# A block inverse in an RWKV-7 and window-attention layer: 64x64 products on all four tiles of TensorE

## What is computed

```python
def wkv_step(S, inp):
    r_t, w_t, k_t, v_t, a_t, b_t = inp
    sa = jnp.einsum('bhij,bhj->bhi', S, a_t)
    S = S * w_t[:, :, None, :] + sa[..., None] * b_t[:, :, None, :] + v_t[..., None] * k_t[:, :, None, :]
    return S, jnp.einsum('bhij,bhj->bhi', S, r_t)
```

## Time and profile before

| | us |
|---|---|
| median of three runs | 1687.83 (1686.51 to 1688.15) |
| the profiled execution | 1689.05 |
| its span, first to last instruction | 1687.0 |
| one step of the heads, j = 3 | 44.3 |
| all nine steps, x of j = 0 to the mean of the last tile | 392.16 |

### The profile page before, as it was taken

The page is one execution under the profiler, slowest core; times in us unless marked ns, Lnnn a source line. Parts: engine busy times, 40 slices in busy tenths (PEclk is TensorE's granted clock), DMA queues, the critical chain, the costliest instruction groups (busy, mean ns, idle before and its releaser), DMA issues. The chain is left out here.

```text
span 1687.0 us, 37211 instructions
## 1 busy us (share of the span) xinstructions
PE 1564.6 (93%) x15821; PEld 1471.5 (87%) x15821; DVE 777.4 (46%) x1310; ACT 579.6 (34%) x1126; POOL 125.4 (7%) x131
## 2 busy tenths in 40 slices
PE   6999998689899998839999999999999999999998
PEld 6999997477777777629988999999999999999998
DVE  5123332567677766362233443333444333344444
ACT  6443211455555555452124222332222233322211
POOL 3000000222222222020000000000000000000000
PEclk9999998799999999959999999999999999999999
DMA  6111111000000000034002111101111111011003
GB/s 177 38 48 39 49 37 33 7 4 3 3 3 3 3 3 3 4 94 126 25 12 89 48 28 51 51 27 47 50 50 36 39 50 50 25 50 50 25 1 106
DMA packets 82531, 66.82 MB, mean 40 GB/s; under 512 B 14929, under 2 KB 74507, under 8 KB 82411
## 3 DMA queue, kind: packets, MB, share of 16 engines
q1 hardware_dynamic: 79939, 64.26, 12.9%
q10 hardware_dynamic: 2408, 0.76, 0.2%
q0 software_dynamic: 64, 0.03, 0.0%
HBM read 59.66 MB, written 5.44 MB: 39 GB/s over the span
## 5 line engine op out<-in xcount | busy, mean ns | idle before, releaser
L100 PE MATMUL bank<-mix_hi,uw_hi 128*128 128x384 f32 (+1 forms) x768 | 255.7, 333 | 6.6 <-DVE uw_lo L1903 6.6
L100 PE MATMUL bank<-u_hi,dw_hi 128*128 128x384 f32 (+1 forms) x768 | 255.5, 333 | 3.6 <-DVE dw_lo L1908 3.6
L1923 DVE TENSOR_TENSOR hT<-hT,bank 128x384 f32<-128x384 f32 (+1 forms) x384 | 197.3, 536 | 131.7 <-PE bank L102 131.7
L101 PE MATMUL bank<-mix_lo,uw_hi 128*128 128x384 f32 (+1 forms) x768 | 255.1, 332 | 0.0
L102 PE MATMUL bank<-mix_hi,uw_lo 128*128 128x384 f32 (+1 forms) x768 | 255.0, 332 | 0.0
L101 PE MATMUL bank<-u_lo,dw_hi 128*128 128x384 f32 (+1 forms) x768 | 253.7, 330 | 0.0
L102 PE MATMUL bank<-u_hi,dw_lo 128*128 128x384 f32 (+1 forms) x768 | 253.6, 330 | 0.0
L1915 DVE TENSOR_TENSOR u_lo<-xn,u_hi 128x384 fp32r<-128x384 f32 (+1 forms) x96 | 52.0, 542 | 308.8 <-ACT u_hi L1874 308.8
L100 PE MATMUL bank<-x_hi,w_hi 128*128 128x384 f32 (+1 forms) x480 | 160.2, 334 | 0.1
L101 PE MATMUL bank<-x_lo,w_hi 128*128 128x384 f32 (+1 forms) x480 | 158.4, 330 | 0.0
L102 PE MATMUL bank<-x_hi,w_lo 128*128 128x384 f32 (+1 forms) x480 | 158.3, 330 | 0.0
(11 more groups left out here) (272 smaller groups left out, 2476.2 us busy)
## 6 DMA issues: line engine op xcount, KB each, us to landing
w_stage<-in_w_up SPq DMA_DIRECT2D x32, 512.0 KB, 4.5
d_stage<-in_w_down SPq DMA_DIRECT2D x32, 512.0 KB, 4.2
w_stage<-in_w_in SPq DMA_DIRECT2D x16, 512.0 KB, 3.9
proj<-in_x SPq DMA_DIRECT2D x9, 512.0 KB, 5.1
xs<-in_x SPq DMA_DIRECT2D x9, 512.0 KB, 4.5
w_stage<-in_w_in SPq DMA_DIRECT2D x8, 256.0 KB, 4.3
w_stage<-in_w_out SPq DMA_DIRECT2D x8, 256.0 KB, 3.1
w_stage<-in_w_out SPq DMA_DIRECT2D x16, 128.0 KB, 4.0
```

Source lines behind the costliest of these rows:

```text
L100: pe.matmul(out, hi, x_hi, start=first, stop=False)
L101: pe.matmul(out, hi, x_lo, start=False, stop=False)
L1923: dve.tensor_tensor(hT[:, m, c:c + n], hT[:, m, c:c + n], bank[j % 6][:, 0:n], ALU.add).then_inc(dn_add.sem, 1)
```

## The change

For half of the heads, a product's result is put on the other half of the partitions than the one it contracts over. So 8 of the 16 matmuls of a product use the two tiles off the array's diagonal, and TURN says which pairs of heads change the half at each level. turned_half, slot and tile_order keep track of where each head then lies and put straight and crossing matmuls in turn. p1 and e1 don't cross (TURN[1] is zero); p2 to p5, e2 to e4 and t1 to t5 do.

A crossing product writes two banks, one for each half that it contracts over (row), 256 columns in each: p(l) to columns 0 to 255 of banks 0 and 1, e(l) to columns 256 to 511 of the same banks, t(l) to banks 2 and 3. Masks and copies then read two banks in one instruction. All other results get other banks, and out_var moves behind extend(4).

```diff
-        bank = [whole.enter_context(nc.psum_tensor(f"bank{b}", [P, 512], F32)) for b in range(8)]
+        psum = whole.enter_context(nc.psum_tensor("psum", [P, 8, 512], F32))
+        bank = [psum[:, b] for b in range(8)]
...
+SCHEDULE = [("x", 6, 0), ("zw", 7, 1), ("za", 4, 1), ("p1", 0, 0), ("tr_a", 5, 0), ("tr_b", 6, 0), ("e1", 0, 0), ("t1", 2, 0),
+            ("s0a", 7, 0), ("s0b", 4, 0), ("vt", 5, 0), ("p2", 0, 0), ("tr_k", 6, 0), ("tr_v", 7, 0), ("e2", 0, 0), ("t2", 2, 0),
+            ("mean", 4, -1), ("p3", 0, 0), ("kk", 5, 1), ("e3", 0, 0), ("t3", 2, 0), ("pt0", 6, 0), ("pm0", 7, 0), ("p4", 0, 0),
+            ("s1a", 4, 0), ("s1b", 5, 0), ("e4", 0, 0), ("t4", 2, 0), ("var", 6, -1), ("o0", 7, 0), ("p5", 0, 0), ("z", 4, 0),
+            ("t5", 2, 0), ("gate", 5, -1), ("pt1", 6, 0), ("pm1", 7, 0), ("wu0", 0, 0), ("wu1", 1, 0), ("ab0", 2, 1), ("ab1", 3, 1),
+            ("q0", 4, 0), ("q1", 5, 0), ("tg0", 6, 0), ("tg1", 7, 0), ("y0", 0, 0), ("y1", 1, 0), ("st0", 2, 0),
+            ("ak0", 3, 1), ("ak1", 4, 1), ("o1", 5, 0), ("st1", 2, 0), ("bon", 3, 1)]
...
+TURN = {1: (0, 0, 0, 0), 2: (0, 0, 1, 1), 3: (0, 1, 1, 0), 4: (1, 1, 0, 0), 5: (1, 0, 0, 1), 6: (0, 0, 0, 0)}
+def turned_half(l, k, e):
+    return e ^ TURN[l][k // 2]
+def slot(crossing, k, row):
+    if not any(crossing):
+        return k
+    return 4 * row + [m for m in range(8) if crossing[m // 2] == crossing[k // 2]].index(k)
+def tile_order(crossing):
+    if not any(crossing):
+        return [(k, e) for k in range(8) for e in range(2)]
+    sides = [[k for k in range(8) if crossing[k // 2] == side] for side in range(2)]
+    return [(ks[n], e) for n in range(4) for ks in sides for e in range(2)]
+def t_crossing(l):
+    return tuple(a ^ b for a, b in zip(TURN[l], TURN[l + 1]))
...
+    def chain_out(name):
+        if name == "p1":
+            return bank[0]
+        if name == "e1":
+            return bank[1]
+        if name[0] == "t":
+            return psum[:, 2:4, 0:256]
+        return psum[:, 0:2, 0:256] if name[0] == "p" else psum[:, 0:2, 256:512]
...
             def product(j, l):
                 f.await_read(pe, "x" if l == 1 else f"e{l - 1}", j)
-                diagonal(j, f"p{l}", lambda k: Ab(j)[:, k, 0], lambda k: X[:, k])
+                f.await_room(pe, f"p{l}", j)
+                for k, e in tile_order(TURN[l]):
+                    mm = pe.matmul(chain(f"p{l}", k, turned_half(l, k, e), e), Ab(j)[half(e), k, 0], x_at(l, k, e), start=True, stop=True)
+                mm.then_inc(f.full(f"p{l}"), 1)
             def extend(j, l):
                 f.await_read(pe, f"p{l}", j)
                 if l == 1:
                     pe.wait_ge(xt1_ok.sem, xt1_ok.n(j))
+                    f.await_read(pe, "bon", j)
+                    if j > 0:
+                        f.await_read(pe, "y1", j - 1)
                 else:
                     f.await_read(pe, f"t{l - 1}", j)
                 if l < 5:
-                    diagonal(j, f"e{l}", lambda k: XT[:, k], lambda k: Pm[:, k])
-                diagonal(j, f"t{l}", lambda k: Pm[:, k], lambda k: XT[:, k])
+                    f.await_room(pe, f"e{l}", j)
+                    for k, e in tile_order(TURN[l]):
+                        mm = pe.matmul(chain(f"e{l}", k, e, turned_half(l, k, e)), xt_at(l, k, e), pm_at(l, k, e), start=True, stop=True)
+                    mm.then_inc(f.full(f"e{l}"), 1)
+                f.await_room(pe, f"t{l}", j)
+                for k, e in tile_order(t_crossing(l)):
+                    mm = pe.matmul(chain(f"t{l}", k, turned_half(l + 1, k, e), turned_half(l, k, e)), pm_at(l, k, e), xt_at(l, k, e),
+                                   start=True, stop=True)
+                mm.then_inc(f.full(f"t{l}"), 1)
...
                 scores(j, 1)
+                extend(j, 4)
                 if j > 0:
                     out_var(j - 1)
-                extend(j, 4)
                 attend(j, 0)
...
             def extended(j, l):
                 if l < 5:
-                    copy_out(f"e{l}", j, X[:], k8(f.bank(f"e{l}")[:]))
-                copy_out(f"t{l}", j, XT[:], k8(f.bank(f"t{l}")[:]))
+                    copy_out(f"e{l}", j, X[:] if l == 1 else X4, spread(f"e{l}", chain_out(f"e{l}")))
+                copy_out(f"t{l}", j, XT4, spread(f"t{l}", chain_out(f"t{l}")))
...
+                    dve.tensor_tensor(dst[:].rearrange("p (b n) t -> p b n t", b=2), spread(name, chain_out(name)),
+                                      lvl[:, l].unsqueeze(1).unsqueeze(1).to_broadcast([P, 2, 4, 64]), ALU.mult).then_inc(f.read(name), 1)
```

More of the change, by code:

```diff
@@ L87, in build_program @@
         s = dict(sem=sem, sb=sb, proj=proj, ident=ident, ones=ones, ones_bd=ones_bd, par=par, eps=eps, last_p=last_p,
-                 w_stage=w_stage, bank=bank, col=col, bias=bias,
+                 w_stage=w_stage, bank=bank, psum=psum, col=col, bias=bias,
                  wkv_out=Count(nc.alloc_semaphore("wkv_out")),
@@ L566, in scalar @@
         act.wait_ge(self.st_t.sem, self.st_t.n(0))
-        act.activation(v["Hs"][:].rearrange("p a b -> p (a b)"), bank[5][:, 0:256], ACT.Copy)
-        act.activation(v["ksm"][:], bank[4][:, 0:80], ACT.Copy).then_inc(self.st_c.sem, 1)
+        act.activation(v["Hs"][:].rearrange("p a b -> p (a b)"), bank[6][:, 0:256], ACT.Copy)
+        act.activation(v["ksm"][:], bank[3][:, 0:80], ACT.Copy).then_inc(self.st_c.sem, 1)
     def tensor(self, pe):
@@ L579, in tensor @@
         for p in range(4):
-            pe.transpose(bank[5][:, 64 * p:64 * p + 64], self.states[:, P * p:P * p + P], ident[0:64, 0:64])
-        pe.transpose(bank[4][:, 0:80], self.ck, ident[0:80, 0:80]).then_inc(self.st_t.sem, 1)
-SCHEDULE = [("x", 4, 0), ("zw", 6, 1), ("za", 7, 1), ("p1", 0, 0), ("tr_a", 3, 0), ("tr_b", 5, 0), ("e1", 1, 0), ("t1", 2, 0),
[6 rows of a table removed]
+            pe.transpose(bank[6][:, 64 * p:64 * p + 64], self.states[:, P * p:P * p + P], ident[0:64, 0:64])
+        pe.transpose(bank[3][:, 0:80], self.ck, ident[0:80, 0:80]).then_inc(self.st_t.sem, 1)
+SCHEDULE = [("x", 6, 0), ("zw", 7, 1), ("za", 4, 1), ("p1", 0, 0), ("tr_a", 5, 0), ("tr_b", 6, 0), ("e1", 0, 0), ("t1", 2, 0),
[6 rows of a table added]
+TURN = {1: (0, 0, 0, 0), 2: (0, 0, 1, 1), 3: (0, 1, 1, 0), 4: (1, 1, 0, 0), 5: (1, 0, 0, 1), 6: (0, 0, 0, 0)}
[12 more added lines that the diff above has]
+    return tuple(a ^ b for a, b in zip(TURN[l], TURN[l + 1]))
 class Fills:
@@ L636, in loop_heads @@
     kst, vtk, vmt, vms, ksm, Lg, PT, PTm, nm, sm, sk = (v[k] for k in "kst vtk vmt vms ksm Lg PT PTm nm sm sk".split())
+    psum = s["psum"]
+    X4, XT4 = (t[:].rearrange("p (b n) t -> p b n t", b=2) for t in (X, XT))
     f = Fills(sem, bank)
@@ L670, in window, with chain, x_at, pm_at @@
         return cols(0) if j == 0 else cols(j, P, -64 if e == 0 else 0)
+    def chain(name, k, out, row):
+        n = slot(t_crossing(int(name[1])) if name[0] == "t" else TURN[int(name[1])], k, row)
+        at = chain_out(name)[half(out)]
+        return at[:, 64 * n:64 * n + 64] if len(at.shape) == 2 else at[:, row, 64 * (n % 4):64 * (n % 4) + 64]
+    def chain_out(name):
[6 more added lines that the diff above has]
+        return psum[:, 0:2, 0:256] if name[0] == "p" else psum[:, 0:2, 256:512]
+    def x_at(l, k, e):
+        return X[half(e), k if l == 1 else slot(TURN[l - 1], k, turned_half(l - 1, k, e))]
+    def pm_at(l, k, e):
+        return Pm[half(turned_half(l, k, e)), slot(TURN[l], k, e)]
+    def xt_at(l, k, e):
+        return XT[half(turned_half(l, k, e)), k if l == 1 else slot(t_crossing(l - 1), k, turned_half(l - 1, k, e))]
+    def spread(name, ap):
+        return k8(ap) if name in ("p1", "e1", "x") else ap.rearrange("p b (n t) -> p b n t", n=4)
     r_in = lambda j: proj[:, 0:4, cols(j)]
@@ L807, in apply @@
                         for e in range(2):
-                            mm = pe.matmul(f.bank(f"wu{g}")[half(e), P * (k % 4):P * (k % 4) + P], XT[half(e), k], AZ[half(e), k],
+                            mm = pe.matmul(f.bank(f"wu{g}")[half(e), P * (k % 4):P * (k % 4) + P], xt_at(6, k, e), AZ[half(e), k],
                                            start=True, stop=True)
@@ L1255, in level @@
                 f.await_full(dve, name, j)
-                dve.tensor_tensor(dst[:], k8(f.bank(name)[:]), lvl[:, l].unsqueeze(1).to_broadcast([P, 8, 64]),
-                                  ALU.mult).then_inc(f.read(name), 1)
+                if name in ("x", "p1"):
+                    dve.tensor_tensor(dst[:], k8(f.bank(name)[:]), lvl[:, l].unsqueeze(1).to_broadcast([P, 8, 64]),
+                                      ALU.mult).then_inc(f.read(name), 1)
+                else:
+                    dve.tensor_tensor(dst[:].rearrange("p (b n) t -> p b n t", b=2), spread(name, chain_out(name)),
+                                      lvl[:, l].unsqueeze(1).unsqueeze(1).to_broadcast([P, 2, 4, 64]), ALU.mult).then_inc(f.read(name), 1)
             def product(j, l):
```

## The result

The changed kernel took 1664.95 us in the median of four runs (1662.17 to 1671.20), the kernel before 1687.73 beside it: ratio 0.9873, 95% interval 0.985 to 0.9895. The forecast was 1659, with 1645 to 1674. The profiled execution is the fastest run, 1662.17 with a span of 1660.0. In it the loop over the nine tiles lasts 363.49 us instead of 392.16: 28.67 less, where the sum said 28.5. So the walk through the steps held in this execution, the fastest of the four, and the question is why the other runs are up to 9 us longer than this one.

A forecast was written before the change was run, and what follows sets the result against it. TensorE was nearest to a bound, in a chain with VectorE and ScalarE. Savings of 1.7 + 7 x 3.2 + 4.4 = 28.5 us took the median of 1687.83 to 1659, range 1645 to 1674.

The forecast's parts named there:

- e2: Product on TensorE in step j = 3, released by VectorE's mask of p2: forecast to start 0.47 us earlier.
- e4: Product on TensorE in step j = 3, starting 0.06 us behind its mask's end: forecast gain 2.84 us.
- the sum: Saving over the nine tile steps: 1.7 first, 7 x 3.2 middle, 4.4 last, 28.5 us in all.
- the walk: Step j = 3 followed wait by wait: of 5.6 us saved on TensorE, 3.2 shorten the step, 2.4 become idle time.
- The banks: New dealing of results to banks in the loop: the new waits are met early, cost 0.
- The two-bank reads: Masks and copies reading two banks in one instruction: taken as 0, at most 1.05 us a step, up to 9 in all.
- out_var's move: Output product placed behind t4: e4 starts 0.06 instead of 0.67 us behind its mask's end.
- (a): Rival: all of TensorE's saving in the loop lands, 50.8 us, giving 1637; chance 0.07.
- (d): Rival: crossing and straight tiles don't overlap when alternating, or two-bank reads eat the gain: about 1687 us; chance 0.04.
- (c): Rival: the clock stays low from the transposes to the gate product's end, 3.4 us slower a step, 1715; chance 0.05.
- (b): Rival: the clock falls after the longer gap before the transposes, 1.5 us a step, 12 in eight, 1671; chance 0.18.
- my case: The prediction's own outcome for the whole kernel: 1659 us, with 1650 to 1668 around it; chance 0.66.

The follow-up runs named there:

- after: The changed kernel itself, no further edit, first measurement: 1664.95 us, ratio 0.9873; its profiled execution is the fastest run, 1662.17 us.
- before_again: The kernel before the change, no edit, one more run: loop 391.52 us, q at 34.29 to 34.36 us in steps 1 to 7.
- no_cross_var: Changed kernel with no product crossing and out_var ahead of extend(4) again, so only the banks are new: 1690.78 us, ratio 1.0011.
- var_back: Changed kernel with out_var put back ahead of extend(4), all else as changed: 1671.31 us, ratio 0.9893.
- straight_first: Changed kernel with each product's eight straight matmuls issued first, then its eight crossing ones: 1679.85 us, ratio 0.9945.
- after_again: The changed kernel measured a second time, no edit: 1669.45 us, ratio 0.9889.
- after_third: The changed kernel measured a third time, no edit: 1667.99 us, ratio 0.9867.
- reorder: Changed kernel with the logits' maximum behind the mask of p2, and softmax work ahead of the next tile's preparation: 1659.12 us, ratio 0.9816.
- filler: Changed kernel with two matmuls on constants in front of the wait before pt0 in every step: 1668.42 us, ratio 0.9885.
- split_logits: Changed kernel with VectorE's maximum of the logits moved behind the mask of p2: 1660.11 us, ratio 0.9829.

## Why the prediction was right, and where it was off

**The walk.** Gains at the points of step 3, each the time of the earlier trace rows less that of after, less the 7.46 us by which the step itself starts earlier:

| point | forecast | measured |
|---|---|---|
| e2 | 0.47 | 0.37 |
| p3 | 1.41 | 1.30 |
| Pm of p3 | 1.87 | 1.72 |
| pt0 (idle there) | 1.87 (2.3) | 1.73 (2.23) |
| Pm of p4 | 2.23 | 2.17 |
| e4 | 2.84 | 2.69 |
| pt1 (idle there) | 3.2 (1.6) | 2.97 (1.52) |
| q | 3.2 | 3.08 |

The small loss sets in at e2: it starts 0.15 behind the end of its mask (450.28 + 0.69 to 451.12), where it started 0.06 behind before, and the same 0.15 stands at e4. I had carried the 0.06 over. By stretches the sum is 2.1 for the first step (forecast 1.7), 7 x 3.14 for the middle (7 x 3.2) and 4.6 for the last (4.4). That it comes within 0.2 of 28.5 is in part luck. Of three profiles of the changed kernel this is the one without a fall, and the first step's 2.1 hangs on when the clock comes up: before_again has 41.79 there instead of 43.07, against which the gain is 0.8.

**The terms at nothing.** The banks: right (no_cross_var: q unchanged). The two-bank reads: right (691 and 592 ns; the earlier trace rows have 0.69 and 0.60), so the upper bound of 1.05 a step didn't come into play. out_var's move is the term whose use I mis-sized: by the walk it takes 0.6 from the way to e4 (0.67 behind the mask, then 0.06). var_back shows the 0.5 at e4 (466.43 is 19.69 behind its step's start, 461.03 of after 19.19), and shows that none of it reaches q where the clock stays up. Without crossing the move costs 0.2.

**The rivals.** (a), all 5.6 a step, fell: 2.4 a step became idle time at the named waits. (d) fell by the product's 0.69, and straight_first shows that its doubt was not empty: in the other order more than half of the gain is gone. (c) didn't happen; the clock came back within 3.5 us in the middle steps.

(b) is the part that I had wrong. Its sign, a granted clock under 1.00 in the loop, stands behind these gaps in two of the three profiles. I set it against my case as all or nothing, 1.5 us in each of eight steps. It is a matter of chance for each gap: 7 of 27 gaps, none in the profile of after, at 0.9 to 1.2 us a time behind pt0. Its price was too high because I doubled the transposes as well: in after_again the clock falls a microsecond behind the gap, and pt0 still takes 0.66. Where pt0 itself was slow (1.12, step 5 of after_third), q came 1.23 late. And I overlooked the gap before pt1 of step 0, where no output product of an earlier tile stands: q is 2.9 to 3.3 later there, 2.7 to 2.8 of it behind pt1. The Trainium skill, TensorE: Matmul & The Clock Gate, section A second HAM failure mode, puts a loss of throughput down to frequent small idles; the rows agree for gaps of 2.2 us. The length of a gap alone doesn't decide. In the loop the 32 gaps of up to 1.46 before the change show no fall; of nine gaps of 1.74 to 1.81 in straight_first one does, of seven of 1.84 to 1.98 in var_back two, of seven of 1.98 in reorder all. Behind the loop, a gap of 1.45 has a fall in the earlier trace rows and none in before_again.

**What is left.** Against the kernel before, run beside them, the three medians of the changed kernel save 22.8, 19.2 and 22.0 us of my 28.5; with the gaps filled it is 25.3, interval 23.1 to 28.2. So filling gave back 2.5 to 6 of the 6 to 9 that are missing, by medians of different chips. In that kernel's profile the loop is 1.6 longer than in the profile of after: the slow start of step 0 (1.1), and a stall in t4 in the last step (0.8 at q). The remaining 1 to 2 us lie in the stalls behind q and outside the loop, where a profiled run's time less its loop is anything from 1295.2 to 1299.6 us in these kernels; which of the two it is stays open.

## What to carry to other kernels

When a product gets shorter, walk the chain from wait to wait: here 5.6 us a step shrank to 3.1, and the walk found each place. Then look at the gaps that the walk itself makes longer: a matrix engine that idles longer may work more slowly afterwards, by chance, and a few matmuls on constants in the gap (1.98 us of work) can pay for themselves; where there is no gap they stand on the chain (1.8 us in filler's last step). A queue in which other work, here the maximum of the logits, stands before the mask that the chain waits for is the next thing to change, as split_logits shows, until that engine is full, as reorder shows.

## What was not expected of the hardware

- Four tiles gave 0.69 us a product with straight and crossing matmuls in turns; with all straight ones first it was 0.98, on two tiles 1.15.
- In straight_first the first matmuls of t (413.59) start before the last of e (413.64), which stand ahead of them in the program. The Trainium skill, TensorE: Matmul & The Clock Gate, section The mechanism, has matmuls start and end in the order of the program; these rows differ from that for the starts. So do rows of the kernel before: in step 3 the scores start at 455.37, the last of t1 at 455.42.
- VectorE's normalisation takes 0.76 alone (457.52) and 1.37 beside GpSimd's kh (467.80), and BB 1.53 in reorder beside GpSimd's product (0.91 in after); the earlier trace rows had shown the normalisation's two lengths already. The 128x4 sum before the second normalisation, 0.15 alone in reorder (509.45), takes 1.01 beside GpSimd's bh in after and ends with it (466.54 + 1.01 and 466.03 + 1.50). Whether a shared port or something else lengthens them, no run here tells apart.
